# 100 early U chunks with one token group each beside 64 of them, low weight parts there by VectorE alone

## The chip, the cores and the metric

One core of a Trainium2 chip runs the whole program. The metric is the device time of one execution in microseconds (us), smaller is better. Five engines work side by side and meet through semaphores: TensorE (PE, matrix products into PSUM), VectorE (DVE), ScalarE (ACT), GpSimd (POOL), and SyncE (SP), which here only issues DMAs.

## The reference

Two transformer blocks run one after the other on 256 tokens (272 keys with the meta tokens) of width 1024, all in float32. The part that the change touches is the PEER layer of the first block, a mixture of 128 x 128 = 16,384 tiny experts:

```
q      = rmsnorm(h) @ w_query                  # 8 heads, two halves of 128
s1, s2 = q1 @ keys1.T, q2 @ keys2.T            # 128 scores each, per head
top 16 of s1, top 16 of s2, top 16 of their 16 x 16 sums -> 16 experts (a, b) and softmax weights per head
out    = sum over chosen experts e of  weight[e] * gelu(h . U[e]) * V[e]
```

The kernel computes it densely. For each b of 128 one chunk of 128 experts gives gelu(U_b h) (128 experts x 256 tokens); that is multiplied by G[:, b, :], the 128 x 128 x 256 table of routing weights (zero where an expert was not chosen), and sent through V_b. Every weight matrix is float32, and a product is made from three products of the operands' high and low parts: w_hi x_hi + w_hi x_lo + w_lo x_hi.

## The kernel before

**Blocks.** All big weights stream through one ring of four slots (RING = 4) as blocks of 128 x 1024 floats (512 KB). For block n SP loads `raw` (`load`, L409), ScalarE copies it to `w_hi` (`hi`, L588), and VectorE or GpSimd forms `w_lo = raw - w_hi` (`lo`, L1043 on VectorE, L487 on GpSimd; `lo_owner`, L106, says which engine owns block n). TensorE then uses the block in 24 matmuls, either projecting (L1643, `project`) or, for V blocks, expanding (L2020, `expand`), and adds to `block_used`. `hi(n)` waits for the load and for block n-4 to be used; `next_load(n)` waits for the low part of block n-4. In the loops below ScalarE is three blocks ahead of TensorE.

**Order of the PEER layer.** TensorE's order is written out by hand, and every other engine follows the same order:

1. Query stage: 16 query blocks alternate with 16 U chunks. `early` on ScalarE (L843) takes each U product through Gelu into a ring `a_out` (the tile kv_mem) of four, and SP stores it to DRAM (`store`, L428). VectorE meanwhile finds the top 16s.
2. Routing tail: EARLY - EARLY_G - 16 = 16 U chunks more (B_EARLY to B_BESIDE) while VectorE finishes the routing (L1339 to L1359). Before the last of them TensorE waits for `route_ready` and transposes the routing tables (L1989); ScalarE copies them to `route_t` (L857), and VectorE waits for that.
3. Beside stage: EARLY_G = 32 U chunks beside the building of G. G is built in 64 groups of four tokens. For a group VectorE makes 4 x 2 one-hot matrices (L1365, L1366, into `one1`, `one2`, double-buffered, in the tile work), TensorE multiplies them (L2003, four products, eight matmul records), and ScalarE copies 128 x 512 of the result into G (L868). There are two groups to one chunk. GpSimd owns all low parts from the query stage to here (`B_QUERY <= n <= B_V`).
4. V stage: EARLY = 64 chunks only expand. Their activations come back from DRAM (`early_back`, L454; the last four lie still in `a_out`), VectorE multiplies by G and splits (L1384, L1391, L1393). Low parts alternate between GpSimd (even blocks) and VectorE (odd blocks).
5. Pair stage: the other 128 - EARLY = 64 chunks, a U projection and a V expansion each.

The second block follows (from L2063), and nothing in it is touched.

**Who waits for whom in the beside stage.** VectorE's group g waits for `g_product`, that group g-2 is multiplied (its buffer). TensorE's group g waits for `one_hot_ready` of g and `g_ready` of g-2 (the PSUM bank is copied out). Its `project` waits for the block's low part and for `bank_free` of the chunk two before. ScalarE's order in a round is its two copies into G, the `hi` of the block three ahead, and then the Gelu of this round's chunk. SP's order is one load (six blocks ahead) and one store.

Of the kernel before, what the change touches and what calls it, by code (L numbers as in the profile page):

```python
# [49 lines left out]
LINE = FAR + NQ + 1  # L50

PH, NKEYS, TOPK = 8, 128, 16
EARLY = 64
SOFT_AT = 5
EARLY_G = 32

MH, GH, GDK, GDV, CHUNK = 8, 4, 32, 64, 64
NCH = NQ // CHUNK
# [47 lines left out]
def lo_owner(n):  # L106

    if B_MEM <= n < B_OUT:
        return None
    return "pool" if B_QUERY <= n <= B_V or n % 2 == 0 else "dve"  # L110


class At:
# [22 lines left out]
def build(nc, dram):  # L136
    ctx = ExitStack()
    with ctx:
# [5 lines left out]
        def sem(name):  # L144
            if name not in sems:
                sems[name] = ctx.enter_context(nc.semaphore(name))
            return sems[name]
# [254 lines left out]
        @block.sync  # L402
        def _(sp):
            sp.dma_start(par[:, :], dram["params"]).then_inc(sem("par_loaded"), 16)

            sp.wait_ge(sem("h_loaded2"), 16)

            def load(n):
                sp.dma_start(raw[:, n.mod(RING), :], dram["blocks"][bass.ds(n.value(), 1)].rearrange("a p c -> p (a c)")  # L409
                             ).then_inc(sem(f"raw_loaded{n.mod(RING)}"), 16)  # L410

            def next_load(n):
                if B_MEM <= n.first - RING < B_OUT:

                    sp.wait_ge(sem("block_used"), n.first - RING + 1)
                else:

                    sp.wait_ge(*rest_taken(n.plus(-RING)))
                load(n)

            def early(w):

                return (w // 2 if w % 2 else None) if w < 4 * PH else w - 2 * PH

            def store(c, m):

                sp.wait_ge(sem("bank_free"), m.value())
                sp.dma_start(early_store[bass.ds(c.value(), 1)].rearrange("a p t -> p (a t)"), a_out[:, c.mod(RING), :]  # L428
                             ).then_inc(sem(f"early_stored{c.mod(RING)}"), 16)

            for j in range(RING):
                load(At(j))
            sp.dma_start(flat2(mem_t[:, :, :]), dram["mem_t"]).then_inc(sem("mem_loaded"), 16)

            for n in range(RING, B_EARLY + LOADS_AHEAD):
                next_load(At(n))
                w = n - LOADS_AHEAD - B_QUERY
                if w >= 0 and early(w) is not None:
                    store(At(early(w)), At(M_QUERY + w + 1))

            with sp.Fori(0, (EARLY - 2 * PH) // RING - 2) as i:
                for j in range(RING):
                    next_load(At(B_EARLY + LOADS_AHEAD + j, i, RING))
                    store(At(2 * PH + j, i, RING), At(M_QUERY + 4 * PH + j + 1, i, RING))
            for j in range(RING):
                next_load(At(B_V - 2 * RING + LOADS_AHEAD + j))
                store(At(EARLY - 2 * RING + j), At(M_PEER - 2 * RING + j + 1))
            for n in range(B_V - RING + LOADS_AHEAD, B_V + RING + 2):
                next_load(At(n))

            def early_back(v):

                c = v.plus(-RING)
                sp.dma_start(a_in[:, v.mod(RING), :], early_store[bass.ds(c.value(), 1)].rearrange("a p t -> p (a t)")  # L454
                             ).then_inc(sem(f"early_loaded{v.mod(RING)}"), 16)


            for j in range(RING):
                sp.wait_ge(sem(f"early_stored{j}"), 16 * (EARLY // RING - 1))
            sp.wait_ge(sem("g_ready"), NQ // 4)  # L460
            for v in range(RING, 2 * RING):
                early_back(At(v))
                if v >= RING + 2:
                    next_load(At(B_V + v))
            for v in range(2 * RING, 2 * RING + 2):
                next_load(At(B_V + v))
            with sp.Fori(0, EARLY // RING - 2) as i:
                for j in range(RING):
                    next_load(At(B_V + RING + LOADS_AHEAD + j, i, RING))

                    sp.wait_ge(sem("act_used"), At(RING + j + 1, i, RING).value())
                    early_back(At(2 * RING + j, i, RING))
            begin = B_PEER + LOADS_AHEAD - RING
            left = N_BLOCKS - begin
            with sp.Fori(0, left // RING) as i:
                for j in range(RING):
                    next_load(At(begin + j, i, RING))
            for n in range(N_BLOCKS - left % RING, N_BLOCKS):
                next_load(At(n))
# [3 lines left out]
        def _(pool):  # L483
            def lo(n):
                pool.wait_ge(sem("hi_done"), n.value(taken(n.first)))
                s = n.mod(RING)
                pool.tensor_tensor(w_lo[:, s, :], raw[:, s, :], w_hi[:, s, :].bitcast(F32), ALU.subtract  # L487
                                   ).then_inc(sem("lo_pool"), 1)
# [65 lines left out]
            los(pool_at[0], B_QUERY + 2)  # L554
            norm_lo(R_PEER, NQ)
            los(B_QUERY + 2, B_QUERY + RING)
            with pool.Fori(1, (B_V - B_QUERY) // RING) as i:
                for j in range(RING):
                    lo(At(B_QUERY + j, i, RING))
            def even(first, end):  # L560

                first += first % 2
                rounds = (end - first) // RING
                with pool.Fori(0, rounds) as i:
                    for j in range(0, RING, 2):
                        lo(At(first + j, i, RING))
                los(first + RING * rounds, end)

            lo(At(B_V))
            even(B_V + 1, B_IN2 + 2)  # L570
            even(B_IN2 + 2, B_OUT2 + 2)
            normalise(U_MOBA, U_X)
            pool_at[0] = B_OUT2 + 2
# [7 lines left out]
        def _(act):  # L581
# [281 lines left out]

            def beside(i):
                for j in range(RING):
                    for g in range(2 * j, 2 * j + 2):
                        act.wait_ge(sem("g_product"), At(g + 1, i, 8).value())
                        act.activation(G[:, :, bass.ds(At(4 * g, i, 32).value(), 4)],  # L868
                                       ps[:, 2 + g % 2, :].rearrange("p (t e) -> p e t", t=4), ACT.Copy
                                       ).then_inc(sem("g_ready"), 1)  # L870
                    hi(At(B_BESIDE + 3 + j, i, RING))
                    early(At(EARLY - EARLY_G + j, i, RING), At(M_PEER - EARLY_G + j, i, RING))

# [157 lines left out]
        def _(dve):  # L1031
# [315 lines left out]
            for half in range(2):  # L1347
# [11 lines left out]
            dve.tensor_tensor(soft_hk, soft_hk, soft_s.rearrange("p a b -> p (a b)").unsqueeze(2).to_broadcast(  # L1359
                [P, 2 * PH, TOPK]), ALU.mult).then_inc(sem("route_ready"), 1)  # L1360

            dve.wait_ge(sem("route_t_ready"), 3)

            def one_hot(g, j, tok):
                dve.tensor_scalar(one1[:, g, j, :], con("iota"), route_t[:, 0, tok], None, ALU.is_equal)  # L1365
                return dve.tensor_scalar(one2[:, g, j, :], con("iota"), route_t[:, 1, tok], route_t[:, 2, tok],  # L1366
                                         ALU.is_equal, ALU.mult)

            for g in range(2):
                for j in range(4):  # L1370
                    ins = one_hot(g, j, slice(4 * g + j, 4 * g + j + 1))
                ins.then_inc(sem("one_hot_ready"), 1)
            with dve.Fori(1, NQ // 8) as i:
                for g in range(2):

                    dve.wait_ge(sem("g_product"), 2 * i + (g - 1))
                    for j in range(4):
                        ins = one_hot(g, j, bass.ds(8 * i + (4 * g + j), 1))
                    ins.then_inc(sem("one_hot_ready"), 1)


            def split(c, a, chunk):
# [25 lines left out]
                dve.wait_ge(sem("gelu_done"), d.plus(1).value())  # L1408
                split(d.plus(EARLY), ge[:, d.mod(2), :], d.plus(EARLY))

            los(B_V + 2)
            dve.wait_ge(sem("g_ready"), NQ // 4)
            for c in range(RING):

# [209 lines left out]
        def _(pe):  # L1624
# [370 lines left out]
            def beside(i, first=False):  # L1995

                for j in range(RING):
                    for g in range(2 * j, 2 * j + 2):
                        pe.wait_ge(sem("one_hot_ready"), At(g + 1, i, 8).value())
                        if not first or g >= 2:  # L2000
                            pe.wait_ge(sem("g_ready"), At(g - 1, i, 8).value())
                        for k in range(4):
                            mm = pe.matmul(ps[:, 2 + g % 2, P * k:P * k + P], one1[:, g % 2, k, :], one2[:, g % 2, k, :],  # L2003
                                           start=True, stop=True)
                        mm.then_inc(sem("g_product"), 1)
                    m = At(M_PEER - EARLY_G + j, i, RING)
                    project(At(B_BESIDE + j, i, RING), m.mod(2), NQ, (sem("bank_free"), m.plus(-1).value()))

# [333 lines left out]
```

## Time and profile before

| | us |
|---|---|
| median of 3 runs | 1537.55 (1532.9 to 1538.8) |
| the profiled execution | 1533.37 |
| its span | 1531.4 |
| TensorE busy | 1436.3 (94%) |
| VectorE busy | 1058.7 (69%) |
| ScalarE busy | 684.4 (45%) |
| GpSimd busy | 678.5 (44%) |
| mean granted TensorE clock | 0.973 |

The profile is of one execution, and times in it count from the span's start. A matmul's record is longer than the distance to the next one, since matmuls are pipelined; rates are read from distances between starts. A wait counts against an engine only where work of that engine ended last in the chain. By stage: the query stage lies at about 242 to 339, the routing tail at 339 to 403, the beside stage at 403 to 593, the V stage at 593 to 774 and the pair stage at 774 to 1136.

### The profile page before, as it was taken

The numbers are of one execution on the slowest core, as the hardware profiler recorded it, in microseconds if no ns is written. First come the engines' busy times: TensorE is split into PE (matmuls) and PEld (weight loads), VectorE is DVE, ScalarE is ACT, GpSimd is POOL, SyncE is SP. The second block draws the span as 40 slices with busy tenths as digits, with TensorE's granted clock in tenths as the row PEclk, the third lists the DMA queues.
The fourth block names the chain that finished last, engine by engine and source line by source line (L and its number), as shares of the span: only waits on it lengthen the run. The fifth ranks groups of instructions, "written<-read, shape, count | busy, mean of one in ns | idle before, by whom it ended". The sixth has DMA issues, their size and how long they took to land.

```text
span 1531.4 us, 31404 instructions
## 1 busy us (share of the span) xinstructions
PE 1436.3 (94%) x11038; PEld 1351.3 (88%) x11038; DVE 1058.7 (69%) x2036; ACT 684.4 (45%) x1035; POOL 678.5 (44%) x300
## 2 busy tenths in 40 slices
PE   7999998998688889999999999999999988999997
PEld 5776588998688889999999999999999967799997
DVE  4424636889899997776665665655655755489997
ACT  4433644444244444333344444444445456555553
POOL 2313247779544434444444444444433425255442
PEclk9999989999799999999999999999999999999999
DMA  7411035666433334777755555565564324255552
GB/s 274 138 55 42 28 124 186 194 191 185 120 117 112 110 120 155 229 230 232 235 183 177 190 183 180 185 188 182 180 198 138 138 69 132 64 191 187 185 176 81
DMA packets 79624, 240.69 MB, mean 157 GB/s; under 512 B 8896, under 2 KB 25552, under 8 KB 78928
## 3 DMA queue, kind: packets, MB, share of 16 engines
q1 hardware_dynamic: 75744, 228.75, 47.3%
q10 hardware_dynamic: 3824, 11.17, 2.0%
q8 instruction: 38, 0.62, 0.2%
q14 instruction: 18, 0.15, 0.0%
HBM read 229.37 MB, written 10.52 MB: 157 GB/s over the span
## 4 chain that ended last, share of the span: by engine, by line
PE 77%; DVE 18%; issue 2%; ACT 1%; DVEq 1%; DMA 0%; POOL 0%; ACTq 0%
PE ps L1643 37%; PE ps L2020 27%; DVE work L1365 6%; DVE work L1366 2%; PE ps L1907 2%; PE ps L1861 1%; PE ps L1658 1%; DVE big L1352 1%; PE ps L1832 1%; DVE big L1350 1%; PE ps L1881 1%; DVE big L1065 1%; DVEq L1366 1%; DVE big L1354 1%; PE ps L2003 1%
## 5 line engine op out<-in xcount | busy, mean ns | idle before, releaser
L487 POOL TENSOR_TENSOR w_lo<-raw,w_hi 128x1024 fp32r<-128x1024 f32 x241 | 626.0, 2600 | 727.9 <-ACT w_hi L588 727.8
L1643 PE MATMUL ps<-x_op,w_hi 128*128 128x256 f32 (+1 forms) x3968 | 746.6, 289 | 20.8 <-DVE x_op L1061 8.8
L1643 PEld LDWEIGHTS ps<-x_op,w_hi 128*128 128x128 f32 x3968 | 627.6, 194 | 34.0 <-issue 20.9
L1643 PE MATMUL ps<-x_op,w_lo 128*128 128x256 f32 (+1 forms) x1984 | 567.5, 286 | 0.0
L588 ACT ACTIVATE w_hi<-raw 128x1024 fp32r<-128x1024 f32 x400 | 420.5, 1055 | 253.0 <-PE ps L2020 201.3
L2020 PE MATMUL ps<-h_op,w_hi 128*128 128x256 f32 x2400 | 428.5, 279 | 2.5 <-DVE h_op L1593 2.5
L1643 PEld LDWEIGHTS ps<-x_op,w_lo 128*128 128x128 f32 x1984 | 385.5, 194 | 0.0
L2020 PEld LDWEIGHTS ps<-h_op,w_hi 128*128 128x128 f32 x2400 | 368.0, 188 | 3.1 <-issue 1.9
L2020 PE MATMUL ps<-h_op,w_lo 128*128 128x256 f32 x1200 | 337.3, 281 | 0.0
L1043 DVE TENSOR_TENSOR w_lo<-raw,w_hi 128x1024 fp32r<-128x1024 f32 x159 | 206.5, 1299 | 103.0 <-ACT w_hi L588 102.9
L2020 PEld LDWEIGHTS ps<-h_op,w_lo 128*128 128x128 f32 x1200 | 225.2, 188 | 0.0
L1365 DVE TENSOR_SCALAR work<-kept,route_t 128x128 f32<-128x128 f32 x256 | 132.3, 517 | 4.6 <-PE ps L2003 2.6
L1393 DVE TENSOR_TENSOR h_op<-work,h_op 128x256 fp32r<-128x256 f32 x128 | 121.9, 952 | 4.4
L1384 DVE TENSOR_TENSOR work<-work,big 128x256 f32<-128x256 f32 x124 | 54.7, 441 | 73.6 <-ACT work L889 72.4
L2003 PE MATMUL ps<-work 128*128 128x128 f32 x512 | 71.2, 283 | 29.3 <-DVE work L1366 29.3
L1391 DVE CAST h_op<-work 128x256 fp32r<-128x256 f32 x128 | 58.5, 457 | 54.0 <-PE ps L2020 45.0
L1366 DVE TENSOR_SCALAR work<-kept,route_t 128x128 f32<-128x128 f32 x256 | 94.9, 371 | 0.0
L2003 PEld LDWEIGHTS ps<-work 128*128 128x128 f32 x512 | 62.9, 193 | 35.2 <-DVE work L1366 35.2
L889 ACT ACTIVATE work<-ps 128x256 f32<-128x256 f32 x64 | 24.7, 386 | 125.1 <-PE ps L1643 125.1
L843 ACT ACTIVATE kv_mem<-ps 128x256 f32<-128x256 f32 x64 | 24.6, 384 | 96.2 <-PE ps L1643 96.2
L868 ACT ACTIVATE big<-ps 128x512 f32 (+1 forms) x64 | 38.2, 598 | 65.3 <-PE ps L2003 65.3
L524 POOL TENSOR_TENSOR big<-big 128x544 f32<-128x544 f32 (+1 forms) x24 | 25.6, 1066 | 81.5 <-DVE big L1230 81.5
(267 smaller groups left out, 1079.8 us busy)
## 6 DMA issues: line engine op xcount, KB each, us to landing
raw<-blocks SPq DMA_DIRECT2D x404, 512.0 KB, 3.5
early_store<-kv_mem SPq DMA_DIRECT2D x60, 128.0 KB, 3.3
work<-early_store SPq DMA_DIRECT2D x60, 128.0 KB, 3.8
big<-consts ACTq DMA_DIRECT2D x2, 1336.0 KB, 6.5
big<-h_t ACTq DMA_DIRECT2D x4, 272.0 KB, 3.7
big<-bias_lines ACTq DMA_DIRECT2D x8, 136.0 KB, 2.8
bias_lines<-route_t ACTq DMA_DIRECT2D x4, 264.0 KB, 3.1
res<-mem_t SPq DMA_DIRECT2D x1, 1024.0 KB, 8.4
```

The source lines that it names most:

```text
L487: pool.tensor_tensor(w_lo[:, s, :], raw[:, s, :], w_hi[:, s, :].bitcast(F32), ALU.subtract).then_inc(sem("lo_pool"), 1)
L588: act.activation(w_hi[:, s, :], raw[:, s, :], ACT.Copy).then_inc(sem("hi_done"), 1)
L868: act.activation(G[:, :, bass.ds(At(4 * g, i, 32).value(), 4)], ps[:, 2 + g % 2, :].rearrange("p (t e) -> p e t", t=4), ACT.Copy).then_inc ...
L1043: dve.tensor_tensor(w_lo[:, s, :], raw[:, s, :], w_hi[:, s, :].bitcast(F32), ALU.subtract).then_inc(sem("lo_dve"), 1)
L1365: dve.tensor_scalar(one1[:, g, j, :], con("iota"), route_t[:, 0, tok], None, ALU.is_equal)
L1366: return dve.tensor_scalar(one2[:, g, j, :], con("iota"), route_t[:, 1, tok], route_t[:, 2, tok], ALU.is_equal, ALU.mult)
L1384: dve.tensor_tensor(hf[:, b, :], a, G[:, bass.ds(chunk.value(), 1), :].rearrange("p e t -> p (e t)"), ALU.mult).then_inc(sem("act_used"), 1)
L1391: dve.tensor_copy(h_op[:, b, 0, :], hf[:, b, :]).then_inc(sem("act_hi"), 1)
L1393: dve.tensor_tensor(h_op[:, b, 1, :], hf[:, b, :], h_op[:, b, 0, :].bitcast(F32), ALU.subtract).then_inc(sem("acts_ready"), 1)
L1643: mm = pe.matmul(ps[:, m_bank, 0:T], w, x, start=(k == 0 and j == 0), stop=(k == last and j == 2))
L2003: mm = pe.matmul(ps[:, 2 + g % 2, P * k:P * k + P], one1[:, g % 2, k, :], one2[:, g % 2, k, :], start=True, stop=True)
L2020: mm = pe.matmul(out, w, x, start=(first and j == 0 and k % 2 == 0), stop=(last and j == 2), skip_group_check=True)
```

## The change

EARLY goes from 64 to 100 and EARLY_G from 32 to 64. The routing tail gets 20 chunks (was 16), the beside stage 64 chunks with one group each (was 32 with two), the V stage 100 (was 64) and the pair stage 28 (was 64). The number of blocks, of groups and of matmuls is the same. From B_BESIDE to B_V + 1 VectorE alone makes the low parts: two before the first group, and then one behind each group's one-hot matrices; GpSimd comes back at B_V + 2. SP unrolls the loads and stores of the routing tail and the first four loads of the pair stage, in the same order as before. `layout` follows from the constants alone.

```diff
-EARLY = 64
+EARLY = 100
-EARLY_G = 32
+EARLY_G = NQ // 4
@@ lo_owner
-    return "pool" if B_QUERY <= n <= B_V or n % 2 == 0 else "dve"
+    if B_QUERY <= n < B_V + 2:
+        return "pool" if n < B_BESIDE else "dve"
+    return "pool" if n % 2 == 0 else "dve"
@@ SP
-            with sp.Fori(0, (EARLY - 2 * PH) // RING - 2) as i:
+            for k in range(B_BESIDE - B_EARLY):
+                next_load(At(B_EARLY + LOADS_AHEAD + k))
+                store(At(2 * PH + k), At(M_QUERY + 4 * PH + k + 1))
+            with sp.Fori(0, EARLY_G // RING - 2) as i:
                 for j in range(RING):
-                    next_load(At(B_EARLY + LOADS_AHEAD + j, i, RING))
-                    store(At(2 * PH + j, i, RING), At(M_QUERY + 4 * PH + j + 1, i, RING))
+                    next_load(At(B_BESIDE + LOADS_AHEAD + j, i, RING))
+                    store(At(EARLY - EARLY_G + j, i, RING), At(M_PEER - EARLY_G + j + 1, i, RING))
...
-            begin = B_PEER + LOADS_AHEAD - RING
+            begin = B_PEER + LOADS_AHEAD
+            for n in range(begin - RING, begin):
+                next_load(At(n))
@@ GpSimd
-            with pool.Fori(1, (B_V - B_QUERY) // RING) as i:
+            with pool.Fori(1, (B_BESIDE - B_QUERY) // RING) as i:
                 for j in range(RING):
                     lo(At(B_QUERY + j, i, RING))
...
-            lo(At(B_V))
-            even(B_V + 1, B_IN2 + 2)
+            even(B_V + 2, B_IN2 + 2)
@@ ScalarE, beside
-                    for g in range(2 * j, 2 * j + 2):
-                        act.wait_ge(sem("g_product"), At(g + 1, i, 8).value())
-                        act.activation(G[:, :, bass.ds(At(4 * g, i, 32).value(), 4)],
-                                       ps[:, 2 + g % 2, :].rearrange("p (t e) -> p e t", t=4), ACT.Copy
-                                       ).then_inc(sem("g_ready"), 1)
+                    act.wait_ge(sem("g_product"), At(j + 1, i, RING).value())
+                    act.activation(G[:, :, bass.ds(At(4 * j, i, 4 * RING).value(), 4)],
+                                   ps[:, 2 + j % 2, :].rearrange("p (t e) -> p e t", t=4), ACT.Copy
+                                   ).then_inc(sem("g_ready"), 1)
                     hi(At(B_BESIDE + 3 + j, i, RING))
                     early(At(EARLY - EARLY_G + j, i, RING), At(M_PEER - EARLY_G + j, i, RING))
@@ VectorE
+            los(B_BESIDE + 2)
             dve.wait_ge(sem("route_t_ready"), 3)
...
-            with dve.Fori(1, NQ // 8) as i:
-                for g in range(2):
-                    dve.wait_ge(sem("g_product"), 2 * i + (g - 1))
+            def groups(i, begun=True):
+                for g in range(RING):
+                    if begun or g >= 2:
+                        dve.wait_ge(sem("g_product"), At(g - 1, i, RING).value())
                     for j in range(4):
-                        ins = one_hot(g, j, bass.ds(8 * i + (4 * g + j), 1))
+                        ins = one_hot(g % 2, j, bass.ds(At(4 * g + j, i, 4 * RING).value(), 1))
                     ins.then_inc(sem("one_hot_ready"), 1)
+                    lo(At(B_BESIDE + 2 + g, i, RING))
+            groups(0, False)
+            with dve.Fori(1, EARLY_G // RING) as i:
+                groups(i)
...
-            los(B_V + 2)
             dve.wait_ge(sem("g_ready"), NQ // 4)
@@ TensorE, beside
-                    for g in range(2 * j, 2 * j + 2):
-                        pe.wait_ge(sem("one_hot_ready"), At(g + 1, i, 8).value())
-                        if not first or g >= 2:
-                            pe.wait_ge(sem("g_ready"), At(g - 1, i, 8).value())
+                    pe.wait_ge(sem("one_hot_ready"), At(j + 1, i, RING).value())
+                    if not first or j >= 2:
+                        pe.wait_ge(sem("g_ready"), At(j - 1, i, RING).value())
...
                     m = At(M_PEER - EARLY_G + j, i, RING)
                     project(At(B_BESIDE + j, i, RING), m.mod(2), NQ, (sem("bank_free"), m.plus(-1).value()))
```

## Rows read from the trace of the kernel before

**Rows 1.** Busy time by engine on the page: us (share of span), instructions.
```profile
PE 1436.3 (94%) x11038; PEld 1351.3 (88%) x11038; DVE 1058.7 (69%) x2036; ACT 684.4 (45%) x1035; POOL 678.5 (44%) x300
```
**Rows 2.** Windows: stretch and length, busy per engine, PEclk, DMA share, GB/s.
```profile
400.00:590.00 190.00, 160.71 (x1283) 154.77 (x1283) 185.66 (x512) 80.49 (x129) 79.34 (x32) 0.98 0.33 107
...
393.00:398.00 5.00, 0.00 (x0) 0.00 (x0) 4.86 (x5) 0.00 (x0) 3.97 (x1) 0.50 0.42 131
398.00:403.00 5.00, 4.66 (x28) 4.66 (x29) 2.95 (x13) 1.15 (x3) 0.00 (x0) 0.65 0.36 105
...
592.68:773.59 180.91, 180.91 (x1538) 180.91 (x1538) 125.27 (x222) 68.35 (x65) 79.66 (x32) 1.00 0.73 226
773.59:1133.29 359.70, 359.70 (x3026) 359.61 (x3026) 217.19 (x251) 149.67 (x188) 158.46 (x63) 1.00 0.59 184
```
**Rows 3.** Chain of waits, 400 to 600: start us, us, what; shares by line first.
```profile
by line: DVE work L1365 44.4%; DVE work L1366 18.8%; issue 12.0%; PE ps L1643 8.4%; DVEq L1366 6.4%; PE ps L2003 4.4%; PE ps L2020 3.7%; DVEq L1365 1.3%; DVEq L1373 0.5%; DVEq L1415 0.0%
...
414.64 4.65 PE ps L1643 x24
419.29 1.78 PE ps L2003 x16
421.07 2.87 PE ps L1643 x24
```
**Rows 4.** Timeline of VectorE, one round of two groups: start us, us, what.
```profile
539.44 2.46 DVE L1365 TENSOR_SCALAR work<-kept,route_t 128x128 f32<-128x128 f32 x1
541.82 0.33 DVE L1366 TENSOR_SCALAR work<-kept,route_t 128x128 f32<-128x128 f32 x1
542.08 0.27 DVE L1365 TENSOR_SCALAR work<-kept,route_t 128x128 f32<-128x128 f32 x1
...
543.88 0.28 DVE L1365 TENSOR_SCALAR work<-kept,route_t 128x128 f32<-128x128 f32 x1
...
545.24 2.48 DVE L1365 TENSOR_SCALAR work<-kept,route_t 128x128 f32<-128x128 f32 x1
```
**Rows 5.** Timeline of all engines in that round; brackets: idle before, and releaser.
```profile
540.16 0.98 PEld L2003 LDWEIGHTS ps<-work 128*128 128x128 f32 x8
540.27 1.05 PE L2003 MATMUL ps<-work 128*128 128x128 f32 x8
540.47 0.38 ACT L843 ACTIVATE kv_mem<-ps 128x256 f32<-128x256 f32 x1 [1.23 <-PE ps L1643]
541.45 0.60 ACT L868 ACTIVATE big<-ps 128x512 f32 x1 [0.60 <-PE ps L2003]
542.21 0.97 PEld L2003 LDWEIGHTS ps<-work 128*128 128x128 f32 x8 [1.08 <-DVE work L1366]
543.99 1.05 ACT L588 ACTIVATE w_hi<-raw 128x1024 fp32r<-128x1024 f32 x1
545.12 2.51 POOL L487 TENSOR_TENSOR w_lo<-raw,w_hi 128x1024 fp32r<-128x1024 f32 x1 [3.30 <-ACT w_hi L588]
```
**Rows 6.** Instructions of one tile or line: ns min/median/max, first and last start.
```profile
L1043 DVE TENSOR_TENSOR w_lo<-raw,w_hi x159: 1148/1218/5445, 23.4 to 1510.1; 128x1024 fp32r<-128x1024 f32 x159
L487 POOL TENSOR_TENSOR w_lo<-raw,w_hi x241: 2344/2487/4437, 12.8 to 1506.5; 128x1024 fp32r<-128x1024 f32 x121
L1350 DVE TENSOR_TENSOR big<-big,kept x4: 2293/4384/4389, 354.7 to 386.0; 128x2048 f32<-128x2048 f32 x4
DMA to landing us min/median/max: 3.1/3.5/8.0
```
**Rows 7.** Timeline of the routing tail: GpSimd, VectorE, TensorE, ScalarE.
```profile
385.96 0.50 PE L1643 MATMUL ps<-x_op,w_hi 128*128 128x256 f32 x2 [1.25 <-POOL w_lo L487]
388.24 8.73 POOL L487 TENSOR_TENSOR w_lo<-raw,w_hi 128x1024 fp32r<-128x1024 f32 x2
390.45 4.31 DVE L1352 TENSOR_TENSOR big<-big 128x2048 f32<-128x2048 f32 x1
397.86 0.43 DVE L1359 TENSOR_TENSOR big<-big 128x256 f32<-128x256 f32 x1
398.34 1.54 PE L1989 MATMUL ps<-kept,big 128*128 128x128 f32 x6 [9.24 <-DVE big L1359]
399.07 1.24 ACT L857 ACTIVATE route_t<-ps 128x256 f32<-128x256 f32 x3 [8.60 <-PE ps L1989]
400.34 0.29 DVE L1365 TENSOR_SCALAR work<-kept,route_t 128x128 f32<-128x128 f32 x1 [2.05 <-ACT route_t L857]
403.35 1.95 PE L2003 MATMUL ps<-work 128*128 128x128 f32 x16
```
**Rows 8.** Chain of waits, whole span: first, the V stage; then a pair.
```profile
592.68 180.91 PE ps L2020 x1536
...
799.41 2.88 PE ps L1643 x24
802.29 2.83 PE ps L2020 x24
```

More of the change, by code:

```diff
@@ L1367, in one_hot @@
                                          ALU.is_equal, ALU.mult)
-            for g in range(2):
-                for j in range(4):
-                    ins = one_hot(g, j, slice(4 * g + j, 4 * g + j + 1))
-                ins.then_inc(sem("one_hot_ready"), 1)
-            with dve.Fori(1, NQ // 8) as i:
-                for g in range(2):
-                    dve.wait_ge(sem("g_product"), 2 * i + (g - 1))
+            def groups(i, begun=True):
+                for g in range(RING):
+                    if begun or g >= 2:
+                        dve.wait_ge(sem("g_product"), At(g - 1, i, RING).value())
                     for j in range(4):
-                        ins = one_hot(g, j, bass.ds(8 * i + (4 * g + j), 1))
+                        ins = one_hot(g % 2, j, bass.ds(At(4 * g + j, i, 4 * RING).value(), 1))
                     ins.then_inc(sem("one_hot_ready"), 1)
+                    lo(At(B_BESIDE + 2 + g, i, RING))
+            groups(0, False)
+            with dve.Fori(1, EARLY_G // RING) as i:
+                groups(i)
             def split(c, a, chunk):
@@ L1997, in beside @@
                 for j in range(RING):
-                    for g in range(2 * j, 2 * j + 2):
-                        pe.wait_ge(sem("one_hot_ready"), At(g + 1, i, 8).value())
-                        if not first or g >= 2:
-                            pe.wait_ge(sem("g_ready"), At(g - 1, i, 8).value())
[L2002 to L2005, printed above, removed]
+                    pe.wait_ge(sem("one_hot_ready"), At(j + 1, i, RING).value())
+                    if not first or j >= 2:
+                        pe.wait_ge(sem("g_ready"), At(j - 1, i, RING).value())
+                    for k in range(4):
+                        mm = pe.matmul(ps[:, 2 + j % 2, P * k:P * k + P], one1[:, j % 2, k, :], one2[:, j % 2, k, :],
+                                       start=True, stop=True)
+                    mm.then_inc(sem("g_product"), 1)
                     m = At(M_PEER - EARLY_G + j, i, RING)
```

## The prediction

> **What bounds the kernel now.** I read the busy shares first: TensorE is busy 94% of the span [rows 1], so a change can only win where TensorE is not. The windows show where that is: from 400 to 590 it is busy for 160.7 of 190 us and VectorE for 185.7, while in the V stage and the pair stage TensorE is busy without a gap at full granted clock [rows 2]. The chain of waits of that stretch names the one-hot lines for 63% of the time, and "issue" (mostly short steps between them) for 12% [rows 3]. The timeline of VectorE says why. A round of two groups takes 545.24 - 539.44 = 5.80 us. Four pairs of one-hot instructions take 543.88 - 542.08 = 1.80 us, eight take 3.6, and the missing 2.2 us are one instruction of 2.46 us whose like take 0.28 [rows 4]. It lies exactly beside GpSimd's low part of 2.5 us [rows 5]: VectorE stands while GpSimd works. That repeats in nearly every round. TensorE needs for a round one projection, 2.87, and two groups, 1.78 [rows 3], so 4.65 of the 5.80. Over the stage, from the first group at 403.4 [rows 7] to the first expansion at 592.7 [rows 8], it needs 32 x 4.65 = 148.8 of 189.3 us: **40.5 us of waiting**, some of it at half clock (a projection of 4.65 instead of 2.87 at 414.64, after a wait) [rows 3].
>
> The Trainium skill ("SBUF — State Buffer", section "SBUF: two separate sides") says that GpSimd and VectorE share a port pair which is locked for a whole instruction, against a VectorE instruction of a two-port mode or with two SBUF inputs. The trace agrees: 2.46 beside 0.28 us [rows 4], and in the routing tail 4.38 us where the least of the same kind is 2.29 [rows 6]. By the rule, taking GpSimd out ends the loss, and VectorE's two early low parts, which have two SBUF inputs, would still shut out GpSimd's last two or wait for them.
>
> **The beside stage after.** Each of the 64 chunks now has on:
>
> - TensorE: one projection 2.87 and one group 1.78 / 2 = 0.89 [rows 3], **3.76 us**;
> - VectorE: four pairs 1.80 [rows 4] and one low part, median 1.22 (least 1.15) [rows 6], 3.02, or 3.2 with two hand-overs of 0.1. The same subtraction is 2.49 on GpSimd [rows 6]; if VectorE needed that much here, a round would be 4.3. Nothing else is on the shared path then, so I take 1.22;
> - ScalarE: 0.60 + 1.05 + 0.38 = 2.03 [rows 5];
> - the DMA queues: 512 + 128 KB, 655 kB in 3.76 us, 174 GB/s. The V stage moves 226 without holding anything up [rows 2].
>
> So TensorE bounds it, unless the new order ties a loop. Low part g+2 stands between the one-hots of g and g+1, and waits for a `hi` that ScalarE issues behind group g-1's copy into G. The loop is: start of group g-1 to the copy's start 541.45 - 540.27 = 1.18, copy 0.60, `hi` 1.05, low part 1.22, one-hots 1.80, group g+1 [rows 4 to 6]: 5.85, with three hand-overs 6.1. It spans two chunks, so 3.1 per chunk, under 3.76. VectorE will stand 0.7 us a round in front of its low part, which costs nothing. The ring has room: a low part ends some 0.3 us into a chunk, the load goes out behind the store at about 1.8, lands 3.5 later (at most 8.0) [rows 6], and its `hi` comes up three chunks on, at 13. The stage takes 64 x 3.76 = **240.6 us**. For each chunk I hold 3.76 to 3.95 possible (a hand-over of 0.1 and the 0.98 of a weight-load train [rows 5] for 0.89): +12 us at most.
>
> At its end VectorE has the last group's copy at about 1.8 us into the last projection and splits the first chunk in 1.2 more, before 2.87 + 0.89 are over; before, too, the expansions began right behind the projection [rows 8].
>
> **The routing tail.** Before, TensorE finishes its 15 projections at 388.8 (the last began at 385.96 behind GpSimd's low part [rows 7]), stands 9.24 us, transposes, projects the 16th at low clock and starts group 0 at 403.4. VectorE's routing ends at 398.3 and GpSimd is busy without a break up to 388.24 + 8.73 = 397.0, being locked out half the time [rows 7]; that much stays, because GpSimd's list is the same up to there. After, 19 projections come before the transposes. Their low parts end at 388.2, 392.6 (halving the 8.73), 397.0, and, free of VectorE, 2.4 later [rows 6] at 399.4; the 20th at 401.8. So TensorE projects 388.8 to 391.7, 392.7 to 395.5, 397.1 to 399.9, 399.9 to 402.8, transposes until 403.5 (six at the 0.12 of a projection's matmul; the 1.54 of the row [rows 7] fell where the granted clock was 0.65 on average [rows 2]), projects the 20th until 406.4. ScalarE's table copies (1.24 [rows 7]) end at 405.1, and VectorE's first one-hots at 406.9. VectorE's two added low parts lie in front of them: the second needs a block whose load waits for the low part that ends at 397.0, 3.5 us to land, then `hi`, so it ends by 404.1, just inside the cover of the table copies. Group 0 starts at **407.1**, 3.7 us later than before, with four more chunks (11.5 us) done. All added work here, the four loads and stores on SP among it, is on blocks that came anyway. Bounds: 406.4 + 0.3 at best; at worst the low parts of 18 and 19 take GpSimd's contended 4.4 each [rows 7] against VectorE's, which shifts it by 4. TensorE stands 1.6 us at most instead of 9.24, after which the granted clock was at its lower level [rows 2, 7]; I reckon with the upper one throughout.
>
> First rounds: `hi` of block B_BESIDE + 2 comes only behind the Gelu of the 20th chunk (406.4 + 0.7, then 1.05), so the low part ends at 409.4 and the one-hots of group 1 at 411.2, where TensorE is ready at 410.8. I add 0.5; between 0 and 3.
>
> **V and pair stage.** 36 chunks move from pairs to expansions alone. An expansion is 180.91 / 64 = 2.83 [rows 8], a pair 359.70 / 63 = 5.71 [rows 2]; the projection that leaves the pair is in the sums above. GpSimd and VectorE share low parts there as before. The first four loads of the pair stage and the handover to GpSimd at B_V + 2 keep their order and cost nothing while SP is six blocks ahead.
>
> **The sum.**
>
> - before: 592.7 + 180.9 + 64 x 5.71 = 1139.0, end of the pair stage;
> - after: 407.1 + 0.5 + 240.6 = 648.2; + 100 x 2.827 = 930.9; + 28 x 5.71 = **1090.8**;
> - difference -48.2.
>
> The rest of the program is untouched. The span goes from 1531.4 to 1483.2, the profiled execution from 1533.4 to 1485.2. That execution lies 4.2 under the median of 1537.55, so the median becomes 1489.4; I say **1489**. As a check from the other side: 40.5 of waiting in the stage goes but for 0.5, and 403.4 - 388.8 = 14.6 with 3.6 of work (11 lost) becomes 18.3 with 15.1 (3.2 lost): 40.0 + 7.8 = 47.8.
>
> **Rivals.**
>
> 1. *VectorE becomes the bound of the beside stage.* If its low part costs what GpSimd's does, or waits and one-hots stretch alike, a round is 4.3: 64 x 0.54 = 35 us more, 1524. For it: VectorE is busy 185.7 of 190 us now [rows 2]. Against: 2.2 of its 5.8 us are standing [rows 4], and no other engine of its path is left. 7 in 100.
> 2. *The loop of four engines closes over one chunk, not two, and the kernel gets slower.* Place: VectorE's low part in front of the next one-hots, waiting for ScalarE's `hi` behind the copy into G. Price: 6.1 us a chunk, 64 x 6.1 = 390 instead of 240.6, 150 more, 1639. It decides from 3.76 + 48.2 / 64 = 4.51 us a chunk on. For it: all four engines now meet once per chunk in a fixed order. Against: one-hots wait for the group before last, there are two PSUM banks and two buffers, and the `hi` is three blocks ahead. 4 in 100.
> 3. *The V stage does not hold 2.83 us over 100 chunks*, because the returned activations are a longer series. At 3.2 a chunk, 37 more, 1526. Against: 64 chunks in one unbroken run at 226 GB/s [rows 2, 8]. 3 in 100.
> 4. *The waiting only moves*: GpSimd's pace in the longer tail (4.4 a block), late loads at the start and a clock that falls again take back most of it: within 8 us of before, about 1535. 3 in 100; all the places I can name add up to 10 us.
>
> **Chances.** The forecast with its own bounds has 83 in 100. Its low end is 1489 less 0.4 and 0.5 for the start and less the 4.7 between the median before and its lowest run: 1483. Its high end is 1489 + 12 + 4 + 3 = 1508. The range 1483 to 1508 leaves the rivals' 17 out. No change means within 0.5%, about 8 us, which is also what a measurement of this kernel can tell. Rivals 1 and 3 are still faster by more than that: faster 93, same 3, slower 4.
>
> **What would show it.** Right: in the beside stage starts of projections 3.76 us apart, TensorE without idle time in front of L2003, no one-hot of over 0.4 us, VectorE idle some 0.7 us before each low part with ScalarE as releaser, no GpSimd work; the first group near 407, the first expansion near 648, the second block's first projection 48 us earlier. Wrong: a distance of 4 us and more with L2003 waiting for VectorE (rival 1, or with VectorE waiting for ScalarE, rival 2), gaps in front of L2020 (rival 3), or a first group after 411.

## The result and the profile after

The changed kernel takes 1490.29 us (median of 4 runs, 1485.42 to 1496.24) against 1535.97 us for the kernel before (4 runs, 1532.9 to 1538.8). The ratio is 0.9705, 95% interval 0.9664 to 0.9746. The forecast was 1489 in a range of 1483 to 1508.

The profiled execution took 1496.24 us, the slowest of the four, with a span of 1494.5. The first line of its page answers to [rows 1]: TensorE is busy as long as before in a shorter span, VectorE 42 us less, GpSimd 121 us less.

```profile
PE 1434.7 (96%) x11038; PEld 1352.7 (91%) x11038; DVE 1016.9 (68%) x2084; ACT 684.3 (46%) x1035; POOL 557.1 (37%) x252
```

The windows (length; busy us of PE, PE weight load, DVE, ACT, POOL; PEclk; DMA share; GB/s) of the beside, V and pair stages answer to [rows 2]. In the beside stage TensorE has no gap, VectorE works 194 of 240.6 us, GpSimd not at all. These are the three windows in that order.

```profile
413.00:653.60 240.60, 240.60 (x2049) 240.60 (x2049) 194.38 (x572) 123.30 (x192) 0.00 (x0) 1.00 0.56 176
653.64:936.40 282.76, 282.76 (x2404) 282.76 (x2403) 195.23 (x348) 106.53 (x101) 123.41 (x50) 1.00 0.75 229
936.40:1090.50 154.10, 154.10 (x1297) 154.01 (x1296) 92.31 (x107) 63.47 (x80) 68.15 (x27) 1.00 0.59 183
```

The chain of waits in the beside stage (start us, us, what) answers to [rows 3]. The one-hot lines are gone from it, and projections start 3.76 us apart.

```profile
by line: PE ps L1651 75.9%; PE ps L2010 23.3%; PE ps L2027 0.9%
...
500.37 2.87 PE ps L1651 x24
504.13 2.87 PE ps L1651 x24
507.89 2.87 PE ps L1651 x24
```

One round in the timeline of all engines, without the projection's matmuls and some one-hots, answers to [rows 4, 5]. The group starts at 533.04, its copy into G at 534.34, the high part at 534.83, the low part at 535.92, and that low part stands before the one-hots of 537.06. VectorE waits 0.73 us for ScalarE before it, and nobody waits for VectorE. Line numbers differ from those before: L1372 and L1373 are the one-hots, L2010 the group, L1049 VectorE's low part, L595 the high part, L874 the copy into G.

```profile
533.04 0.98 PEld L2010 LDWEIGHTS ps<-work 128*128 128x128 f32 x8
...
533.30 0.28 DVE L1372 TENSOR_SCALAR work<-kept,route_t 128x128 f32<-128x128 f32 x1
533.50 0.34 DVE L1373 TENSOR_SCALAR work<-kept,route_t 128x128 f32<-128x128 f32 x1
...
534.34 0.60 ACT L874 ACTIVATE big<-ps 128x512 f32 x1 [0.60 <-PE ps L2010]
...
534.83 1.05 ACT L595 ACTIVATE w_hi<-raw 128x1024 fp32r<-128x1024 f32 x1
...
535.92 1.23 DVE L1049 TENSOR_TENSOR w_lo<-raw,w_hi 128x1024 fp32r<-128x1024 f32 x1 [0.73 <-ACT w_hi L595]
536.80 0.98 PEld L2010 LDWEIGHTS ps<-work 128*128 128x128 f32 x8
```

All one-hots of the changed kernel (ns least/median/greatest) stay under 0.35 us:

```profile
L1372 DVE TENSOR_SCALAR work<-kept,route_t x256: 273/279/287, 410.7 to 647.5; 128x128 f32<-128x128 f32 x128
L1373 DVE TENSOR_SCALAR work<-kept,route_t x256: 333/340/348, 410.9 to 647.7; 128x128 f32<-128x128 f32 x128
```

**Where the time went.** Executions differ by several us in parts that the change does not touch, so I compare by landmarks: the first long instruction of the routing (L1350, after the change L1356), the first group, the first expansion, and the gate product of the second block (L2068, L2075), each by its first start in the per-line answers. Those of after:

```profile
L1356 DVE TENSOR_TENSOR big<-big,kept x4: 2294/4382/4399, 359.7 to 391.1; 128x2048 f32<-128x2048 f32 x4
L2010 PE MATMUL ps<-work x512: 270/275/348, 412.8 to 650.5; 128*128 128x128 f32 x171
L2027 PE MATMUL ps<-h_op,w_hi x2400: 277/280/387, 653.5 to 1481.9; 128*128 128x256 f32 x185
L2075 PE MATMUL ps<-big x2: 374/426/478, 1110.5 to 1110.9; 16*128 16x256 f32 x2
```

| distance, us | before | after |
|---|---|---|
| start to routing landmark | 354.7 | 359.7 |
| to first group | 48.7 | 53.1 |
| to first expansion | 189.1 | 240.7 |
| to gate product | 561.3 | 457.0 |
| **routing landmark to gate product** | **799.1** | **750.8** |
| gate product to end | 377.6 | 384.0 |

The touched part became 48.3 us shorter. The two outer parts were 5.0 and 6.4 us longer in this one execution, which is why its span fell by 36.9 only. The other three runs have spans of 1483.5 to 1488.5, and the medians differ by 45.7.

### The profile page after: what moved, and what is told of

The parts are those of the page before. It is cut to its first block, busy times and chain, and to the rows that moved or that the text cites. A ratio compares the mean times of both kernels' runs of the same rounds, so it can differ in the third digit from the quotient of the medians.

```text
span 1494.5 us, 31410 instructions
## 1 busy us (share of the span) xinstructions
PE 1434.7 (96%) x11038; PEld 1352.7 (91%) x11038; DVE 1016.9 (68%) x2084; ACT 684.3 (46%) x1035; POOL 557.1 (37%) x252
## 4 chain that ended last, share of the span: by engine, by line
PE 80%; DVE 6%; POOL 6%; issue 5%; ACT 1%; DMA 0%; ACTq 0%; POOLq 0%; DVEq 0%
PE ps L1651 37%; PE ps L2027 28%; POOL w_lo L494 6%; PE ps L2010 4%; PE ps L1915 2%; PE ps L1869 2%; PE ps L1666 1%; PE ps L1889 1%; PE ps L1840 1%; DVE big L1071 1%; DVE w_lo L1049 1%; PE ps L1730 1%; PE ps L1761 0%; ACT w_hi L595 0%; DVE big L1063 0%
## 5 line engine op out<-in xcount | busy, mean ns | idle before, releaser
L494 POOL TENSOR_TENSOR w_lo<-raw,w_hi 128x1024 fp32r<-128x1024 f32 x193 | 504.5, 2617 | 804.7 <-ACT w_hi L595 804.7
L595 ACT ACTIVATE w_hi<-raw 128x1024 fp32r<-128x1024 f32 x400 | 420.5, 1055 | 266.5 <-PE ps L2027 214.4
L1049 DVE TENSOR_TENSOR w_lo<-raw,w_hi 128x1024 fp32r<-128x1024 f32 x207 | 265.4, 1282 | 114.2 <-ACT w_hi L595 114.0
L1400 DVE CAST h_op<-work 128x256 fp32r<-128x256 f32 x128 | 69.3, 541 | 80.8 <-PE ps L2027 72.6
L850 ACT ACTIVATE kv_mem<-ps 128x256 f32<-128x256 f32 x100 | 38.4, 384 | 141.3 <-PE ps L1651 141.3
L1373 DVE TENSOR_SCALAR work<-kept,route_t 128x128 f32<-128x128 f32 x256 | 87.0, 340 | 0.0
L1402 DVE TENSOR_TENSOR h_op<-work,h_op 128x256 fp32r<-128x256 f32 x128 | 81.3, 635 | 4.4
L1372 DVE TENSOR_SCALAR work<-kept,route_t 128x128 f32<-128x128 f32 x256 | 71.5, 279 | 0.0
L2010 PE MATMUL ps<-work 128*128 128x128 f32 x512 | 67.4, 274 | 1.1 <-DVE work L1373 1.1
L2010 PEld LDWEIGHTS ps<-work 128*128 128x128 f32 x512 | 62.5, 191 | 1.2 <-issue 1.2
L874 ACT ACTIVATE big<-ps 128x512 f32 (+1 forms) x64 | 38.3, 598 | 36.9 <-PE ps L2010 36.9
L1583 DVE SCALAR_TENSOR_TENSOR big<-big,par 128x255 f32<-128x255 f32 x88 | 47.1, 556 | 7.6 <-ACT big L1004 1.5
```

The costliest lines, as they stand in the source:

```text
L595: act.activation(w_hi[:, s, :], raw[:, s, :], ACT.Copy).then_inc(sem("hi_done"), 1)
L1049: dve.tensor_tensor(w_lo[:, s, :], raw[:, s, :], w_hi[:, s, :].bitcast(F32), ALU.subtract).then_inc(sem("lo_dve"), 1)
L1400: dve.tensor_copy(h_op[:, b, 0, :], hf[:, b, :]).then_inc(sem("act_hi"), 1)
L1402: dve.tensor_tensor(h_op[:, b, 1, :], hf[:, b, :], h_op[:, b, 0, :].bitcast(F32), ALU.subtract).then_inc(sem("acts_ready"), 1)
L1583: dve.scalar_tensor_tensor(out=buf[:, p.mod(2), back:NQ], in0=up_out[:, half, p.mod(2), 0:NQ - back], scalar=par[:, bass.ds(p.value(a + 6 ...
L2010: mm = pe.matmul(ps[:, 2 + j % 2, P * k:P * k + P], one1[:, j % 2, k, :], one2[:, j % 2, k, :], start=True, stop=True)
```

## The experiments

Ten further runs followed, two of them repeats of the changed kernel and of the kernel before. The table gives the distances between the same landmarks; its last column is the sum of the three before it.

| kernel | median us | first group | to expansion | to gate | landmark to gate |
|---|---|---|---|---|---|
| before | 1535.97 | 48.7 | 189.1 | 561.3 | 799.1 |
| changed | 1490.29 | 53.1 | 240.7 | 457.0 | 750.8 |
| changed, again | 1491.51 | 53.0 | 240.7 | 457.7 | 751.4 |
| GpSimd's low parts | 1504.45 | 56.3 | 254.0 | 457.9 | 768.2 |
| alternating low parts | 1495.96 | 54.1 | 240.7 | 457.1 | 751.9 |
| two groups, VectorE's low parts | 1498.59 | 47.4 | 153.0 | 561.1 | 761.5 |
| 96 early | 1496.92 | 47.5 | 241.6 | 469.2 | 758.3 |
| 104 early | 1488.75 | 64.5 | 240.8 | 446.0 | 751.3 |
| loop over one chunk | 1644.05 (one run) | 56.5 | 389.8 | 458.7 | 905.0 |
| SP's tail list in a loop | 1490.07 | 53.0 | 240.7 | 457.6 | 751.3 |
| before, SP's list written out | 1538.25 | 48.7 | 189.1 | 561.4 | 799.2 |
| before, again | 1535.48 (one run) | 48.6 | 189.0 | 561.3 | 798.9 |

Between the routing landmark and the gate product the distances repeat within 0.7 us where the order of work is the same (the three kernels without the change, and the three with it), far closer than whole times do. Outside these landmarks they do not: the stretch behind the gate product took 384.0, 377.6 and 377.6 us in those three with the change.

**The changed kernel again.** No edit.

> The changed kernel once more. Theory: its profiled execution was slow in parts that the change does not touch: the routing's first long instruction (L1356) began at 359.7 us against 354.7 before, and the part behind the pair stage took 5.8 us more than before. If that is the run and not the change, this execution's L1356 begins at 354 to 356, the stage from group 0 to the first expansion again takes 240.8, and the span is 1484 to 1489. Rival: the change itself delays what comes before it (a longer program, SP's unrolled lists): L1356 again begins near 359.7 and the span is 1494.

The touched part came out at 751.4, the stage at 240.7, and the part behind the gate product at 377.6, as before the change: the 6.4 us there were that one execution's. But the routing landmark came at 361.7, late again and not at the 354 to 356 of the theory, and the span was 1490.7, above its 1484 to 1489. On that point the rival stands so far (see SP's list, the last experiments).

**GpSimd makes the low parts, otherwise as changed.**

```diff
 # against the changed kernel; ScalarE's and TensorE's rounds as there
-    if B_QUERY <= n < B_V + 2:
-        return "pool" if n < B_BESIDE else "dve"
-    return "pool" if n % 2 == 0 else "dve"
+    return "pool" if B_QUERY <= n <= B_V or n % 2 == 0 else "dve"
```

> 100 early chunks, 64 of them with one group each, but GpSimd makes the low parts of the beside stage as before. Theory: GpSimd's low part shuts VectorE out for 2.2 us per chunk, so VectorE needs 1.80 + 2.2 = 4.0 us a chunk against TensorE's 3.76: 64 x 0.24 = 15 us more than the changed kernel, about 1505. Rival 1: once TensorE has 3.76 us of work per chunk the owner of the low parts no longer matters: same time as the changed kernel, 1490. Rival 2: the new order is what gained nothing and VectorE's ownership gained all: near the kernel before, 1530.

SP, GpSimd and VectorE keep their lists of the kernel before here; the loop on SP alone changes nothing measurable (see below). 1504.45 (ratio to before 0.9795, 0.9756 to 0.9834) against 1505 expected, and 254.0 / 64 = 3.97 us a chunk: the theory's 4.0. Both rivals fall: the owner still matters (1490 would have said no), and the new order does gain (1530 would have said no). The timeline of VectorE and GpSimd shows the stall of [rows 4] once per chunk, the two instructions starting together:

```profile
540.36 0.27 DVE L1364 TENSOR_SCALAR work<-kept,route_t 128x128 f32<-128x128 f32 x1
540.56 2.52 DVE L1365 TENSOR_SCALAR work<-kept,route_t 128x128 f32<-128x128 f32 x1
540.57 2.42 POOL L487 TENSOR_TENSOR w_lo<-raw,w_hi 128x1024 fp32r<-128x1024 f32 x1 [1.38 <-ACT w_hi L588]
```

And the timeline of TensorE's weight loads (in brackets idle before, and releaser) shows how a deficit of 0.2 us a chunk (3.97 against 3.76) looks: no small wait in each round, but a long one every eighth chunk (31.8 us), when the two buffers are used up.

```profile
455.28 0.97 PEld L2001 LDWEIGHTS ps<-work 128*128 128x128 f32 x8 [1.63 <-DVE work L1365]
487.06 0.97 PEld L2001 LDWEIGHTS ps<-work 128*128 128x128 f32 x8 [1.63 <-DVE work L1365]
518.87 0.97 PEld L2001 LDWEIGHTS ps<-work 128*128 128x128 f32 x8 [1.66 <-DVE work L1365]
```

**Low parts alternate in the beside stage.**

```diff
-    if B_QUERY <= n < B_V + 2:
-        return "pool" if n < B_BESIDE else "dve"
+    if B_QUERY <= n < B_BESIDE:
+        return "pool"
     return "pool" if n % 2 == 0 else "dve"
@@ VectorE, behind each group
-                    lo(At(B_BESIDE + 2 + g, i, RING))
+                    n = At(B_BESIDE + 2 + g, i, RING)
+                    if lo_owner(n.first) == "dve":
+                        lo(n)
@@ GpSimd
-            even(B_V + 2, B_IN2 + 2)
+            even(B_BESIDE, B_IN2 + 2)
```

> As the changed kernel, but in the beside stage low parts alternate, even blocks by GpSimd and odd ones by VectorE, as in the V stage. Theory: over two chunks VectorE needs 3.6 of one-hots + 1.22 + 2.2 of being shut out = 7.0 us, under TensorE's 7.52: the stage still takes 241 us and the time is that of the changed kernel within 2 us, so VectorE alone is not needed. Rival: a chunk in which GpSimd shuts VectorE out comes late for the next group, since the double buffer does not smooth over two chunks: 3.9 on average, 9 us more.

The stage takes 240.7 us again, with TensorE busy throughout and VectorE at 223 of it:

```profile
413.70:654.40 240.70, 240.70 (x2048) 240.70 (x2049) 223.00 (x540) 123.23 (x191) 78.35 (x32) 1.00 0.54 174
```

The rival falls: VectorE need not own every block, half of them is enough. The median of 1495.96 is 4.5 above the changed kernel run beside it, more than the 2 us expected, but the intervals against before (0.9686 to 0.9777 and 0.967 to 0.9766) overlap nearly whole. The touched part is 0.5 to 1.1 longer; the first group came 1.0 to 1.1 later (54.1). So the stage is shown to be the same; that the whole time is, is not shown closer than the noise.

**Two groups per chunk as before, VectorE alone makes the low parts.**

```diff
-EARLY = 100
-EARLY_G = NQ // 4
+EARLY = 64
+EARLY_G = 32
@@ VectorE
-                for g in range(RING):
+                for g in range(2 * RING):
...
-                    lo(At(B_BESIDE + 2 + g, i, RING))
+                    if g % 2:
+                        lo(At(B_BESIDE + 2 + g // 2, i, RING))
```

> The kernel before (64 early chunks, 32 of them with two groups each), with only the owner changed: VectorE alone makes the low parts of the beside stage. Theory: a round needs 3.6 + 1.22 = 4.85 with hand-overs on VectorE against 4.65 on TensorE, so about 4.9 instead of 5.80: 32 x 0.9 = 29 us less, and some 4 us less at the start of the stage, about 1504. Rival: VectorE now waits in each round for ScalarE's high part behind two copies into G, and a round stays at 5.3 or more: 16 us less, about 1520.

1498.59 (0.9749, 0.9711 to 0.9787), 5 us better than expected. The stage gave 36.1 us and not 29, the stretch before it 1.3 and not 4. A round is 153.0 / 32 = 4.78, a little under the theory's 4.9 and far under the rival's 5.3. VectorE is now what bounds it, and its timeline has no idle time in a round, from 499.88 over the low part to 504.64 (4.76 us, where TensorE needs 4.65).

```profile
499.88 0.27 DVE L1373 TENSOR_SCALAR work<-kept,route_t 128x128 f32<-128x128 f32 x1
...
503.24 0.33 DVE L1374 TENSOR_SCALAR work<-kept,route_t 128x128 f32<-128x128 f32 x1
503.50 1.21 DVE L1050 TENSOR_TENSOR w_lo<-raw,w_hi 128x1024 fp32r<-128x1024 f32 x1
504.64 0.27 DVE L1373 TENSOR_SCALAR work<-kept,route_t 128x128 f32<-128x128 f32 x1
```

Of the 48.3 us the owner alone brings 37.6, the order alone (GpSimd's low parts, four more chunks in the tail) 30.9. They do not add, since both remove the same waiting.

**96 and 104 early chunks.** `EARLY = 96` and `EARLY = 104` instead of 100, nothing else.

> The changed kernel with 96 early chunks instead of 100, so that the routing tail has 16 chunks, as before the change. Theory: four projections (11.5 us) come back out of the cover of VectorE's routing, and group 0 starts 5.5 us earlier after the routing's L1356 than with 20 chunks (the kernel with two groups and VectorE's low parts had 47.4 us there, the changed one 53.0): 6 us more in all, about 1496. Rival: the tail is bound by GpSimd's low parts, so the four chunks cost the same wherever they lie: no difference from the changed kernel.

> The changed kernel with 104 early chunks, 24 of them in the routing tail. Theory: with 20 chunks TensorE no longer waits for the routing, and four more only move from the pair stage to the tail at the same 2.87 us: group 0 starts 11.5 us later after L1356, the sum to the end of the pair stage stays at 736 us within 1.5, time as the changed kernel. Rival: there is waiting left in the tail that more chunks fill: 3 us or more less.

With 96 the touched part is 758.3, 7.2 more than the mean 751.1 of the changed kernel's two profiles (the expectation said 6, the prediction's own count 7.8); 0.9 of it lies in the beside stage, which the expectation had left out. TensorE waits 7.2 us in one piece for the end of the routing, and the window at the end of the tail shows it busy 7.8 of 15 us at a granted clock of 0.66:

```profile
392.00:407.00 15.00, 7.79 (x47) 7.59 (x46) 13.39 (x16) 2.48 (x5) 1.49 (x1) 0.66 0.52 158
```

With 104 the first group comes 11.5 us later and the rest is 11.3 shorter: 751.3, no change. Both theories held. Twenty chunks are enough to keep TensorE at work until the routing ends. What waiting is left in the tail is for GpSimd, and more chunks don't fill it; its row in the waits of 104 from 340 to 430 (total us, times, longest) reads:

```profile
PE ps L1651 <- POOL w_lo L494: 7.2, 7, 1.3
```

Its median of 1488.75 (0.9679, 0.9639 to 0.9719) is the lowest of all, but not told apart from the changed kernel's.

Together with the experiment before, this takes the 48 us apart in steps. The new owner alone brings 37.6. One group beside each chunk, with the tail still at 16 chunks, adds 761.5 - 758.3 = 3.2, and the four chunks more in the tail add the 7.2. Once VectorE makes the low parts, most of what the new order still brings comes from the tail.

**The loop closed over one chunk.** Low parts made one block further on.

```diff
-            los(B_BESIDE + 2)
+            los(B_BESIDE + 3)
...
-                    lo(At(B_BESIDE + 2 + g, i, RING))
+                    if not end or g < RING - 1:
+                        lo(At(B_BESIDE + 3 + g, i, RING))
```

> The changed kernel with VectorE's low part in each round made for one block further on (three low parts before the first group, then block B_BESIDE + 3 + g behind the one-hots of group g). It then waits for the high part that ScalarE makes behind the copy of the very same group, and the next one-hots stand behind it. Theory: the loop of four engines closes over one chunk. From the trace of the changed kernel: weight load of the group 416.76, copy into G 417.69, high part 418.18, low part 419.27, one-hots 420.41 to 422.27: 5.6 us a chunk instead of 3.76, 64 x 1.84 = 118 more, about 1608. Rival: the double buffers carry it and a chunk stays at 3.8: about 1490.

One run, 1644.05. The loop closes, and a chunk takes 389.8 / 64 = 6.09 us. That is more than the 5.6 expected here and what the prediction had for its rival 2 (6.1). The timeline (weight load of the group, copy, high part, low part, next group) shows who waits for whom. Two things make the difference to 5.6. The copy now begins 1.29 us after the weight load (509.41 - 508.12) and not the 0.93 that the expectation read, so a round at full granted clock takes 5.86 to 5.95 (the loads of 422.73, 428.59, 434.45 and 440.39). And TensorE idles in each round, after which the granted clock falls at times to its lower level: it is 0.90 over 500 to 620, some groups take 1.51 instead of 0.97, and the round from 501.52 takes 6.60.

```profile
501.52 1.51 PEld L2012 LDWEIGHTS ps<-work 128*128 128x128 f32 x8 [2.13 <-DVE work L1373]
...
503.45 0.60 ACT L874 ACTIVATE big<-ps 128x512 f32 x1 [3.44 <-PE ps L2012]
503.95 1.05 ACT L595 ACTIVATE w_hi<-raw 128x1024 fp32r<-128x1024 f32 x1
505.03 1.23 DVE L1049 TENSOR_TENSOR w_lo<-raw,w_hi 128x1024 fp32r<-128x1024 f32 x1 [3.56 <-ACT w_hi L595]
508.12 0.97 PEld L2012 LDWEIGHTS ps<-work 128*128 128x128 f32 x8 [1.24 <-DVE work L1373]
...
509.41 0.60 ACT L874 ACTIVATE big<-ps 128x512 f32 x1 [1.90 <-PE ps L2012]
```

So the slower outcome was real and one block of distance away: the same instructions, one index shifted, cost 154 us.

**SP's list of the tail: in a loop again, and written out in the kernel before.** The cut shows the first run's edit; the second puts SP's whole part of the change into the kernel before, and the third is the kernel before without an edit.

```diff
-            for k in range(B_BESIDE - B_EARLY):
+            with sp.Fori(0, (B_BESIDE - B_EARLY) // RING - 1) as i:
+                for j in range(RING):
+                    next_load(At(B_EARLY + LOADS_AHEAD + j, i, RING))
+                    store(At(2 * PH + j, i, RING), At(M_QUERY + 4 * PH + j + 1, i, RING))
+            for k in range(B_BESIDE - B_EARLY - RING, B_BESIDE - B_EARLY):
```

> The changed kernel with SP's first 16 load and store pairs of the routing tail in a loop again instead of written out; same order of work. So far every kernel with the list written out (four executions) reached L1356 of the routing at 359 to 362 us with a granted clock of 0.57 to 0.61 in the stretch 100 to 110, and the two without it at 354.5 to 354.7 with 0.83. Theory: the length of SP's program shifts the early phase by a fraction of a microsecond, and that decides where the clock falls: with the loop L1356 starts near 354.6 and the time is 4 to 5 us lower, 1486. Rival: it is chance or another part of the change, and L1356 starts at 359 to 362 again.

> The kernel before with SP's part of the change alone: the loads and stores of the routing tail and the first four loads of the pair stage written out, in the same order; nothing else changed. Theory: SP's list costs nothing, the time is that of the kernel before within its spread; where L1350 of the routing begins (354.5 to 362 in the executions so far) is a matter of where in the attention stage the clock falls, which differs from program to program and run to run. Rival: the written-out list itself delays the early phase by 4 to 5 us: L1350 begins at 359 or later, and the time is 1540.

> The kernel before, unchanged, once more. Theory: its L1350 began at 354.7 by chance, and this execution can lie anywhere from 354.5 to 362. Rival: this program always reaches it at 354.5 to 354.8, so that a part of the change moves the early phase.

With the loop the landmark came at 357.5, which neither side had said, and the median of 1490.07 is that of the changed kernel, not 1486. In the kernel before, the written-out list gave 361.5 in the profile, as its rival had it, but the rival's price did not come: 1538.25 against 1537.53 in 10 and 13 runs, ratio 1.000 (0.9984 to 1.0017), so it costs less than 3 us. The kernel before, again, gave 357.2: it does not always lie at 354.5 to 354.8. The profiled executions do lie in two groups (359.4 to 361.7 in eight with the list written out, 354.5 to 357.5 in four without), and the granted clock of the stretch 100 to 110, in the attention stage, goes with it (0.56 to 0.65 against 0.67 to 0.83). That window in the kernel before with the list written out, and in the kernel before itself:

```profile
100.00:110.00 10.00, 10.00 (x53) 10.00 (x53) 0.35 (x1) 1.49 (x4) 0.00 (x0) 0.56 0.18 52
```
```profile
100.00:110.00 10.00, 10.00 (x69) 9.64 (x69) 0.35 (x1) 1.85 (x5) 0.00 (x0) 0.83 0.17 52
```

Whether SP's list has a part in where the clock falls stays open: the profiles, one for each run, point to it, and the timed runs show no price.

## Why the prediction was right

1. *GpSimd's low part shuts VectorE out for 2.2 us, and that is the waiting.* Shown from both sides: without it no one-hot lasts over 0.35 us and the old order gains 36.1 us in the stage, and with it in the new order the stage takes 13.3 us more.
2. *3.76 us a chunk, 240.6 for the stage.* Measured 240.7. Neither VectorE's low part (1.22, measured 1.23 among the one-hots) nor the 0.2 us that I held possible for hand-overs came to stand on TensorE.
3. *The loop spans two chunks.* Right, and so were the 0.7 us that VectorE would wait (0.73). The price of the one-chunk loop (6.1 a chunk, measured 6.09) is right in its base and partly lucky in its number: the 5.85 of the sum is what a round at full granted clock took (5.86 to 5.95), but of the three hand-overs of 0.1 at most a third shows there, and the rest came from rounds in which the clock fell.
4. *The tail.* I had the first group 3.7 us later; it came 4.3 to 4.4 later. Being shut out for a whole instruction happened in one more place: the routing's last instruction (L1359 before, 0.43 us [rows 7]) met a low part of GpSimd that was not there before and took 1.78. VectorE's first early low part met the last one of GpSimd as foreseen, and took 1.39 instead of 1.22.

```profile
402.96 1.78 DVE L1365 TENSOR_TENSOR big<-big 128x256 f32<-128x256 f32 x1
406.70 1.39 DVE L1049 TENSOR_TENSOR w_lo<-raw,w_hi 128x1024 fp32r<-128x1024 f32 x1 [1.96 <-ACT w_hi L595]
409.58 1.22 DVE L1049 TENSOR_TENSOR w_lo<-raw,w_hi 128x1024 fp32r<-128x1024 f32 x1 [1.49 <-ACT w_hi L595]
```

That stall itself was covered, as TensorE came to the transposes only at 408.0. What stood at the end was the second early low part, 409.58 to 410.8. It ended 0.4 us behind the table copies and not 1 us ahead of them as forecast, so that TensorE waited 1.05 us for the first one-hots. I had counted the load of its block and its high part, but not ScalarE's order: that high part stands behind the Gelu of the 19th chunk (in ScalarE's timeline below, L850 and L595), which ends only after TensorE's 19th projection.

```profile
408.21 0.38 ACT L850 ACTIVATE kv_mem<-ps 128x256 f32<-128x256 f32 x1 [1.55 <-PE ps L1651]
408.50 1.05 ACT L595 ACTIVATE w_hi<-raw 128x1024 fp32r<-128x1024 f32 x1
```

5. *The clock.* It stayed at the upper level through the tail (1.00 in 400 to 413), and the six transposes took 0.82 us instead of 1.54.
6. *V and pair stage.* 282.8 us for 100 chunks against 282.7 reckoned; the longer series of returned activations changed nothing (229 GB/s).
7. *The sum.* 48.2 forecast, 48.3 in the touched part of the profiled execution, 47.7 in the second. That it fits this closely is in part luck: the first group came 0.6 to 0.7 us later than forecast, and the 0.5 us added for the first rounds stayed out (240.7 for the stage instead of 241.1). The median fell by 45.7, and the difference of 2.5 us from the forecast lies within the spread of either kernel.

What the prediction took for a result of VectorE owning every low part is in part a result of the order: at 3.76 us of TensorE work per group, half of the low parts could stay with GpSimd. And while VectorE owns them, the order needs no help from it: the longer tail is what it adds (7.2 of 10.4 us).

## What to carry to other kernels

Before moving work between VectorE and GpSimd, look for single instructions that last as long as one of the other engine. The price of a GpSimd instruction was here nearly its own length on VectorE's path (2.2 of 2.4 us), and two cures worked: to take it away, or to give TensorE enough work per round to cover most of it. When one engine's order is changed by hand, write down the loop through all engines and count how many rounds it spans; here one index decided between 3.76 and 6.09 us. To judge a local change in a long program, compare distances between landmarks around it: here they repeated within 0.7 us where whole times spread over 10.

## What the hardware showed that I had not expected

- A small deficit behind a double buffer shows as one long wait at rare intervals (1.6 us every 31.8 us for 0.2 us a chunk), which a look at single rounds would have missed.
- VectorE's reductions were not slowed beside GpSimd: in the routing tail, where GpSimd worked 39.8 of 40 us, the two-input instructions of 128x2048 took 4.38 us beside GpSimd's low parts against 2.29 for the least, the reductions of the same 2048 elements 2.29 each time. The Trainium skill ("SBUF — State Buffer", section "Who interferes with whom") says the same of `tensor_reduce` on this chip.
- Untouched parts of the program moved by up to 7 us from execution to execution, and the granted clock in short stretches of the attention stages moved with them: 0.56 to 0.83 in 100 to 110, and, in the second block from 1200 to 1280, 0.82 to 0.83 in the execution that took 384.0 behind the gate product against 0.91 in the one that took 377.6. A change of 0.3% (some 5 us) would need the landmarks to be seen.
